# A dense expert stage: the last weight grid stored by halves of its tokens, and plain fp32 output products in its first eight rounds

## The chip, the cores and the metric

The kernel runs on one NeuronCore of one Trainium2 chip. The metric is the device time of one execution in microseconds (us). Engines are named as in the profile: PE (TensorE matmuls), PEld (its weight loads), DVE (VectorE), ACT (ScalarE), POOL (GpSimd), SP (SyncE, which here only issues transfers).

## What is computed

One layer of a hybrid backbone for 1024 latent and 256 context tokens: attention, a gated recurrence, and then a feed-forward layer of product-key experts (PEER). Only the last part is touched. It is, for x of 1280 tokens by 1024:

```
def peer_ffn(x, w_q, sub_keys, u, v):
    ...
    expert = (idx1 * N_KEYS + idx2).reshape(N, PEER_HEADS * PEER_TOPK)
    g = jax.nn.softmax(best, axis=-1).astype(x.dtype).reshape(N, PEER_HEADS * PEER_TOPK)
    def one_chunk(args):
        x_c, e_c, g_c = args
        act = jax.nn.gelu(jnp.einsum('cd,ced->ce', x_c, u[e_c]), approximate=False)
        return jnp.einsum('ce,ced->cd', g_c * act, v[e_c])
```

Each token picks 8 x 16 = 128 of 128 x 128 = 16384 experts. u and v hold one row of 1024 fp32 for each expert.

## The kernel before

The kernel treats tokens in tiles of 128. Four tiles (512 tokens) go the **dense** way: every token is multiplied with all 16384 experts, and a grid of weights, mostly zero, makes the sum right. The other six tiles go the **gathered** way: for each of a token's 128 experts, POOL gathers a row of u (512 KB for 128 tokens), DVE takes the dot product with x, and later a row of v is gathered and multiplied in. Both ways run side by side in `experts`.

`place_weights` makes the dense grid: for each of four tiles t, in 8 steps of 16 tokens, 128 x 128 products on PE, copied by ACT into `grid[t % 2]` (64 KB per partition, partition = first key). A full tile (8 MB) is stored to the scratch tensor g in DRAM; `placed` counts ACT's copies, 32 for a tile. Tiles 0 to 2 are stored by SP (L2177), each when its tile is complete. The last tile is stored when complete: keys 0 to 3 by SP (L2179, semaphore `g_first`), keys 4 to 127 by ACT (L2170, `g_rest`). The block ends with a barrier over all engines, before which SP waits for the stores whose buffers are to be reused.

`experts` runs 64 rounds and an end. Round r treats experts n = 2r and 2r + 1 of each partition (a **pair**, e = 0, 1):

- PE: two products A (24 matmuls each, `a_ps`, L2395), each 8 slices k in three parts (hi x hi, hi x lo, lo x hi) of numbers that were split into two fp32r halves; then the output product O of the pair of round r - 1 (L2417), token tile by token tile, t = 0 to 3, into two PSUM buffers `o_ps[t % 2]`, also in three parts: 12 matmuls a tile.
- ACT: the high halves of v (L2455) and u (L2435), the Gelu of A into `hidden` (L2460), the high half of the weighted hidden, w (L2463).
- DVE: `weigh` (hidden times g_raw, L2635), the low halves of u and v (`split`, L2541) and of w (L2640), the additions of the four O tiles into `acc` (`add_tile`, L2657), and between these the dot products (L2580). The order is written out by hand: round r adds tiles 2 and 3 of O(r - 2) at its start and tiles 0 and 1 of O(r - 1) at its end. PE waits for `added` before it overwrites a PSUM buffer, so O's tile 2 waits for the addition of tile 0.
- SP, in order: v (2r), u (2r + 2), v (2r + 1), g_raw (r), u (2r + 3), 512 KB each. A load of v waits for the split of the v before in the same buffer (`v_ready`), g for both `weigh` of the round before (`weighted`), u for the split of the u before.
- POOL: the gathers; a row's buffer is free after its dot product.

Rounds 0 to 7 have mode "keys": 12 dot products each, over 4 rows of `key_row` and, from round 1 on, 8 of `value_row`. Rounds 8 to 63 have 8 gathered keys (or values) and 8 gathered value rows each, which PE multiplies in (L2381). In round 1, ACT, DVE, POOL and SP wait for `g_rest`, because the buffers of round 1 lie where `grid1` lay.

In what follows, T is the moment in which DVE has added tile 0 of O(r - 1), at the end of round r.

## Time and profile before

| | us |
|---|---|
| median of 3 runs | 3499.54 |
| lowest, highest | 3494.69, 3509.21 |
| span of the profiled execution | 3554.5 |

The profiled execution is 55 us (1.6%) longer than the median. All durations below are from it. Its first 1661 us lie before `experts`; the keys rounds end at 1917.0; rounds 8 to 63 take the time up to about 3510, and a closing normalisation the rest. The profile gives for each engine the busy time and, for each idle stretch, what ended it. Matmuls are pipelined: one of 512 columns is listed with 0.39 us but starts 0.227 us after the last.

### The profile page before, as it was taken

Reading aid. Unit: us, or ns where it says so; the run is one execution under the profiler, and the core shown is the slowest. Engines: PE = TensorE matmul, PEld = TensorE weight load, DVE = VectorE, ACT = ScalarE, POOL = GpSimd, SP = SyncE. Lnnn points to the kernel's source line nnn. Section 1 sums busy time; section 2 is a strip of 40 time slices with the busy share of each in tenths; the row PEclk is TensorE's granted clock in tenths of the full one; section 3 lists DMA queues with packets and bytes.
Section 4 is the critical chain, followed back from the end, with each engine's and each line's share of the span. In section 5 each row is a group of like instructions: output and inputs, shape, how many; then the busy total and the mean of one; then the engine's idle time right before and its main releaser. Section 6 shows DMA issues by size and latency. Waiting matters only on the chain. (4 is left out here: it accounts for less than half of the span.)

```text
span 3554.5 us, 46828 instructions
## 1 busy us (share of the span) xinstructions
PE 3102.6 (87%) x15159; PEld 2086.1 (59%) x15159; DVE 2701.3 (76%) x5989; ACT 1072.9 (30%) x1920; POOL 1925.0 (54%) x1678
## 2 busy tenths in 40 slices
PE   6879999589889996676588999999899999999994
PEld 4647346366464443565466666667676667666663
DVE  2328788797578998898688778777787778787777
ACT  4731344365111110677122222222222222222222
POOL 0000466454345566553665667677667666766673
PEclk9979999799999998898799999999999999999997
DMA  9432788776867889799988999999999999999996
GB/s 331 155 123 74 239 273 263 209 228 208 313 237 244 298 297 327 248 404 340 358 325 299 389 397 385 403 410 399 368 405 401 403 385 410 393 409 378 369 394 261
DMA packets 366664, 1133.22 MB, mean 319 GB/s; under 512 B 33017, under 2 KB 91641, under 8 KB 366385
## 3 DMA queue, kind: packets, MB, share of 16 engines
q0 software_dynamic: 221184, 805.40, 60.5%
q1 hardware_dynamic: 136832, 314.44, 23.9%
q10 hardware_dynamic: 8496, 11.50, 0.9%
q8 instruction: 78, 1.28, 0.1%
q14 instruction: 74, 0.60, 0.1%
HBM read 1077.51 MB, written 53.71 MB: 318 GB/s over the span
## 5 line engine op out<-in xcount | busy, mean ns | idle before, releaser
L403 POOL DMA_INDIRECT ahead_row<-in_u_rows,keep_tables x256 | 339.1, 1325 | 669.8 <-POOLq L102 371.7
L2525 POOL DMA_INDIRECT exp_value_row<-in_v_rows,exp_v_id x448 | 585.0, 1306 | 169.7 <-issue 140.0
L2514 POOL DMA_INDIRECT edge_row<-in_u_rows,edge_u_id x424 | 459.2, 1083 | 345.1 <-DVE edge_dot L2580 165.0
L2417 PE MATMUL exp_o_ps<-exp_v_hi,exp_w_hi 128*128 128x512 f32 x1024 | 337.5, 412 | 104.2 <-DVE keep_acc L2657 101.0
L2395 PE MATMUL exp_a_ps<-exp_xT_hi,exp_u_hi 128*128 128x512 f32 x1024 | 409.0, 399 | 20.8 <-DVE exp_u_lo L2541 11.0
L2395 PE MATMUL exp_a_ps<-exp_xT_lo,exp_u_hi 128*128 128x512 f32 x1024 | 402.0, 393 | 0.5 <-issue 0.3
L2395 PE MATMUL exp_a_ps<-exp_xT_hi,exp_u_lo 128*128 128x512 f32 x1024 | 401.4, 392 | 0.8 <-issue 0.8
L2580 DVE CUSTOM_DVE_ANT_0 edge_row<-edge_row,keep_tables 128x1024 f32<-128x1024 f32 x256 | 313.2, 1224 | 103.6 <-DMA edge_row<-in_u_rows,edge_u_id 81.7
L2657 DVE TENSOR_TENSOR keep_acc<-exp_o_ps,keep_acc 128x1024 f32<-128x1024 f32 x256 | 312.0, 1221 | 94.8 <-PE exp_o_ps L2417 78.6
L413 DVE CUSTOM_DVE_ANT_0 ahead_row<-ahead_row,ahead_x 128x1024 f32<-128x1024 f32 x256 | 305.9, 1220 | 84.6 <-DMA ahead_row<-in_u_rows,keep_tables 83.6
L2417 PE MATMUL exp_o_ps<-exp_v_lo,exp_w_hi 128*128 128x512 f32 x1024 | 327.5, 402 | 0.0
L2417 PE MATMUL exp_o_ps<-exp_v_hi,exp_w_lo 128*128 128x512 f32 x1024 | 325.7, 400 | 0.0
L2417 PEld LDWEIGHTS exp_o_ps<-exp_v_hi,exp_w_hi 128*128 128x128 f32 x1024 | 194.4, 196 | 198.1 <-DVE keep_acc L2657 152.1
L2580 DVE CUSTOM_DVE_ANT_0 edge_row<-edge_row,edge_x 128x1024 f32<-128x1024 f32 x168 | 204.7, 1223 | 69.5 <-DMA edge_row<-in_u_rows,edge_u_id 57.8
L2395 PEld LDWEIGHTS exp_a_ps<-exp_xT_hi,exp_u_hi 128*128 128x128 f32 x1024 | 193.8, 189 | 108.2 <-issue 47.5
L2381 PE MATMUL exp_v_ps<-exp_value_row,exp_hot 128*32 128x512 f32 x1792 | 219.0, 600 | 40.0 <-DMA exp_value_row<-in_v_rows,exp_v_id 20.0
L2455 ACT ACTIVATE exp_v_hi<-exp_v_raw 128x1024 fp32r<-128x1024 f32 x128 | 135.0, 1055 | 381.8 <-PE exp_o_ps L2417 225.6
L2460 ACT ACTIVATE exp_hidden<-exp_a_ps 128x512 f32<-128x512 f32 x128 | 76.6, 599 | 562.8 <-PE exp_a_ps L2395 448.4
L1483 PE MATMUL queries_q_ps<-mix_featT,queries_slab 128*128 128x512 f32 (+1 forms) x640 | 231.1, 514 | 0.0
L2417 PEld LDWEIGHTS exp_o_ps<-exp_v_lo,exp_w_hi 128*128 128x128 f32 x1024 | 199.8, 195 | 44.8
L2417 PEld LDWEIGHTS exp_o_ps<-exp_v_hi,exp_w_lo 128*128 128x128 f32 x1024 | 199.1, 194 | 44.2
L2395 PEld LDWEIGHTS exp_a_ps<-exp_xT_hi,exp_u_lo 128*128 128x128 f32 x1024 | 193.8, 189 | 43.4 <-issue 1.8
(420 smaller groups left out, 5716.2 us busy)
## 6 DMA issues: line engine op xcount, KB each, us to landing
exp_v_raw<-in_v_rows SPq DMA_DIRECT2D x128, 512.0 KB
edge_u_raw<-in_uT SPq DMA_DIRECT2D x128, 512.0 KB
exp_g_raw<-scratch_g SPq DMA_DIRECT2D x64, 512.0 KB
scratch_g<-place_grid SPq DMA_DIRECT2D x3, 8192.0 KB
proj_ctx_mod_slab<-in_w_mod SPq DMA_DIRECT2D x8, 2048.0 KB, 13.2
heads_early_room<-in_w_in SPq DMA_DIRECT2D x10, 1024.0 KB, 11.8
mod_slab<-in_w_mod SPq DMA_DIRECT2D x4, 2048.0 KB, 21.3
queries_slab<-in_w_q SPq DMA_DIRECT2D x4, 2048.0 KB, 26.2
```

What stands on the lines that cost most here:

```text
L403: nc.gpsimd.indirect_dma_start(out=ahead.row[:, n % KEY_RING, :], out_offset=None, in_=io["u_rows"], in_offset=bass.IndirectOffsetOnAxis(a ...
L413: nc.vector.tensor_tensor_reduce(out=row, in0=row, in1=ahead.x[:, n // SLOTS - ahead.first, :], scale=1.0, scalar=0.0, op0=ALU.mult, op1=A ...
L1483: last = nc.tensor.matmul(q_ps[:, 0:width], slab[:, k, ct * P:(ct + 1) * P], h2T[:, k, at:at + width], start=(k == 0), stop=(k == KD - 1))
L2381: mm = nc.tensor.matmul(v_ps[QUAD * t:QUAD * (t + 1), half * SLAB:(half + 1) * SLAB], hot[:, i % 2, t, :], value_row[:, 4 * (i % 2) + t, h ...
L2395: mm = nc.tensor.matmul(a_ps[e][:, :], u[part][:, e, k, :], xT[xp][:, k, :], start=(k == 0 and part == 0 and xp == 0), stop=(k == KD - 1 a ...
L2417: mm = nc.tensor.matmul(o_ps[t % 2][:, c, :], w[1 - parity][part][:, e, t * P:(t + 1) * P], v[1 - parity][xp][:, e, c * SLAB:(c + 1) * SLA ...
L2455: nc.scalar.activation(v[parity][0][:, e, :], v_raw[:, e, :], ACT.Copy).then_inc(v_hi_ready, 1)
L2460: nc.scalar.activation(hidden[:, e, :], a_ps[e][:, :], ACT.Gelu).then_inc(hidden_ready, 1)
L2514: nc.gpsimd.indirect_dma_start(out=row, out_offset=None, in_=io["u_rows"] if mode != "last" else io["v_rows"].rearrange("a b n -> (a b) n" ...
L2525: nc.gpsimd.indirect_dma_start(out=value_row[:, 4 * (j % 2) + t, :], out_offset=None, in_=io["v_rows"].rearrange("a b n -> (a b) n"), in_o ...
L2580: nc.vector.tensor_tensor_reduce(out=row, in0=row, in1=x, scale=1.0, scalar=0.0, op0=ALU.mult, op1=ALU.add, accum_out=dot[:, parity, j:j + ...
L2657: nc.vector.tensor_tensor(acc[:, t, :], o_ps[t % 2][:, :, :].rearrange("p c n -> p (c n)"), acc[:, t, :], ALU.add).then_inc(added, 1)
```

## The change

Four things are changed together.

1. **The last tile's grid is stored by halves of its tokens.** Within a grid the order of elements is now (pair r, half of tokens h, e, token), and for the last tile (h, r, e, token). SP stores tokens 0 to 63 after half of the last tile's copies, as 512-byte pieces; after the last copy, tokens 64 to 127 go out, pairs 0 and 1 by SP, the rest by ACT. SP also waits for the first half's store (`half_stored`) ahead of the barrier.
2. **Buffers are laid out anew.** What rounds 0 to 7 use lies outside the second half of `grid1`; the buffers first used in round 8 (v_raw, the low halves) lie over it. The waits for `g_rest` of ACT, DVE and POOL in round 1 are gone; SP's stays, after the loads of round 1.
3. **The output products of rounds 0 to 7 are plain fp32.** v is loaded to `v_whole[parity]`, `weigh` writes `w_whole[parity]`, and O has 4 plain matmuls a tile in place of 12 fp32r ones. The splits of v and w fall away in these rounds. SP's load of v waits, from round 2 on, for `o_made >= 4 (r - 1)`: for all four tiles of O(r - 2), which read the same buffer.
4. The first A product waits for the slices of xT one by one, and the zeroing of `acc` moves behind the first `weigh`.

```diff
-FIRST_KEYS = 4
-REST_KEYS = ((FIRST_KEYS, N_KEYS),)
+FIRST_PAIRS = 2
...
+            sp.wait_ge(placed, LAST_TILE * PER_TILE + PER_TILE // 2)
+            sp.dma_start(half_target(0, 0, N_KEYS // 2), half_grid(0, 0, N_KEYS // 2)).then_inc(half_stored, 16)
             sp.wait_ge(placed, DENSE_TILES * PER_TILE)
-            sp.dma_start(place(DENSE_TILES - 1, 0, FIRST_KEYS), placed_keys(1, 0, FIRST_KEYS)).then_inc(edge.g_first, 16)
+            sp.dma_start(half_target(1, 0, FIRST_PAIRS), half_grid(1, 0, FIRST_PAIRS)).then_inc(edge.g_first, 16)
             sp.wait_ge(stored[0], 32)
             sp.wait_ge(stored[1], 16)
+            sp.wait_ge(half_stored, 16)
...
                 for e in range(PAIR):
                     n = 2 * r + e
-                    if at_least(r, 1):
+                    if mode == "keys":
+                        if e == 0 and at_least(r, 2):
+                            sp.wait_ge(o_made, DENSE_TILES * (r - 1))
+                        target = v_whole[parity][:, e, :]
+                    else:
                         sp.wait_ge(v_ready, n - 1)
-                    sp.dma_start(v_raw[:, e, :], io["v_rows"][:, n, :]).then_inc(v_in[e], 16)
+                        target = v_raw[:, e, :]
+                    sp.dma_start(target, io["v_rows"][:, n, :]).then_inc(v_in[e], 16)
...
-            pe.wait_ge(xT_ready, 1)
...
+                            if isinstance(r, int) and n == 0:
+                                pe.wait_ge(xT_ready, k + 1)
...
+                            for c in range(2) if whole else ():
+                                mm = nc.tensor.matmul(
+                                    o_ps[t % 2][:, c, :], w_whole[1 - parity][:, e, t * P:(t + 1) * P],
+                                    v_whole[1 - parity][:, e, c * SLAB:(c + 1) * SLAB], start=(e == 0), stop=(e == 1))
...
-                if isinstance(r, int) and r == 1:
-                    act.wait_ge(edge.g_rest[0], 16)
...
-                        if isinstance(r, int) and r == 1 and j == RING:
-                            pool.wait_ge(edge.g_rest[0], 16)
...
                 def split_v(e):
-                    if not last:
+                    if not last and not wide:
```

On PE, behind the A products of round 1, the output product of round 0 (4 token tiles). Before, one tile of the four is six rows of two matmuls:

```order
712 L2417 MATMUL exp_o_ps<-exp_v_hi,exp_w_hi 128x512 x2
713 L2417 MATMUL exp_o_ps<-exp_v_lo,exp_w_hi 128x512 x2
714 L2417 MATMUL exp_o_ps<-exp_v_hi,exp_w_lo 128x512 x2
715 L2417 MATMUL exp_o_ps<-exp_v_hi,exp_w_hi 128x512 x2
716 L2417 MATMUL exp_o_ps<-exp_v_lo,exp_w_hi 128x512 x2
717 L2417 MATMUL exp_o_ps<-exp_v_hi,exp_w_lo 128x512 x2
```

Now the four tiles together are one row, between the last A matmul and the loop:

```order
710 L2423 MATMUL exp_a_ps<-exp_xT_hi,exp_u_lo 128x512
...
712 L2456 MATMUL exp_o_ps<-exp_whole_v,exp_whole_w 128x512 x16
713 L2296 UNCONDITIONAL_BRANCH
```

48 matmuls of split operands have become 16 plain ones.

On DVE, a keys round of the loop from the fourth dot product (a dot product is two rows, ISA) to the second u split. Before:

```order
2292 L2635 TENSOR_TENSOR exp_hidden<-exp_hidden,exp_g_raw 128x512
2293 L2580 ISA exp_value_row,edge_dot<-exp_value_row,edge_x 128x1024
...
2295 L2640 TENSOR_TENSOR exp_w_lo<-exp_hidden,exp_w_hi 128x512
2296 L2541 TENSOR_TENSOR exp_u_lo<-edge_u_raw,exp_u_hi 128x1024
...
2304 L2541 TENSOR_TENSOR exp_v_lo<-exp_v_raw,exp_v_hi 128x1024
...
2306 L2635 TENSOR_TENSOR exp_hidden<-exp_hidden,exp_g_raw 128x512
...
2309 L2640 TENSOR_TENSOR exp_w_lo<-exp_hidden,exp_w_hi 128x512
2310 L2541 TENSOR_TENSOR exp_u_lo<-edge_u_raw,exp_u_hi 128x1024
```

and now:

```order
2282 L2676 TENSOR_TENSOR exp_whole_w<-exp_hidden,exp_g_raw 128x512
2283 L2621 ISA exp_value_row,edge_dot<-exp_value_row,edge_x 128x1024
...
2285 L2585 TENSOR_TENSOR exp_u_lo<-edge_u_raw,exp_u_hi 128x1024
...
2293 L2676 TENSOR_TENSOR exp_whole_w<-exp_hidden,exp_g_raw 128x512
...
2296 L2585 TENSOR_TENSOR exp_u_lo<-edge_u_raw,exp_u_hi 128x1024
```

The two splits of w and the two of v are gone (the first split of v stood further ahead); nothing else has moved.

On SP, from the stores to the loads of round 0. Before:

```order
91 L2177 DMA scratch_g<-place_grid 128x64x256 x3
92 L2179 DMA scratch_g<-place_grid 128x2x256
93 L102 UNCONDITIONAL_BRANCH
```

and now, with the half of the last tile as a row of its own:

```order
91 L2193 DMA scratch_g<-place_grid 128x64x256 x3
92 L2195 DMA scratch_g<-place_grid 128x64x128
93 L2197 DMA scratch_g<-place_grid 128x2x128
94 L102 UNCONDITIONAL_BRANCH
```

The loads of each round behind them stand in the same order as before (v, u, v, g, u), the first of each round now behind the wait for `o_made`.

## Rows read from the trace of the kernel before

**Rows 1.** Page: span, and busy time of each engine.
```profile
span 3554.5 us, 46828 instructions
PE 3102.6 (87%) x15159; PEld 2086.1 (59%) x15159; DVE 2701.3 (76%) x5989; ACT 1072.9 (30%) x1920; POOL 1925.0 (54%) x1678
```
**Rows 2.** Busy time by stretch: rounds 2 to 7, round 8, later rounds.
```profile
core 0: us, PE busy (x) PEld busy (x) DVE busy (x) ACT busy (x) POOL busy (x), PEclk, DMA share, GB/s
1746.30:1917.00 170.70, 143.46 (x578) 115.76 (x577) 152.53 (x217) 39.56 (x54) 106.19 (x79) 0.92 0.85 315
...
1917.00:1944.30 27.30, 26.67 (x116) 20.34 (x116) 21.95 (x33) 6.59 (x9) 15.46 (x15) 0.92 1.02 404
...
2100.00:3300.00 1200.00, 1135.63 (x5504) 818.20 (x5504) 928.25 (x1285) 278.81 (x387) 828.08 (x773) 0.99 1.00 396
```
**Rows 3.** Timeline, ACT: the Gelu of the dots, which ends rounds 0, 1, 7.
```profile
1705.70 0.21 ACT L2470 ACTIVATE edge_act_row<-edge_dot 128x12 f32<-128x12 f32 x1 [7.82 <-DVE edge_dot L2580]
...
1746.32 0.21 ACT L2470 ACTIVATE edge_act_row<-edge_dot 128x12 f32<-128x12 f32 x1 [5.76 <-DVE edge_dot L2580]
...
1917.03 0.21 ACT L2470 ACTIVATE edge_act_row<-edge_dot 128x12 f32 x1 [5.84 <-DVE edge_dot L2580]
```
**Rows 4.** Timeline, DVE, end of round 4 and round 5.
```profile
1831.40 1.22 DVE L2657 TENSOR_TENSOR keep_acc<-exp_o_ps,keep_acc 128x1024 f32<-128x1024 f32 x1
1835.93 1.23 DVE L2657 TENSOR_TENSOR keep_acc<-exp_o_ps,keep_acc 128x1024 f32<-128x1024 f32 x1 [3.30 <-PE exp_o_ps L2417]
...
1841.10 1.22 DVE L2541 TENSOR_TENSOR exp_v_lo<-exp_v_raw,exp_v_hi 128x1024 fp32r<-128x1024 f32 x1
...
1845.67 0.69 DVE L2635 TENSOR_TENSOR exp_hidden<-exp_hidden,exp_g_raw 128x512 f32<-128x512 f32 x1
...
1847.42 0.69 DVE L2640 TENSOR_TENSOR exp_w_lo<-exp_hidden,exp_w_hi 128x512 fp32r<-128x512 f32 x1
...
1858.36 1.22 DVE L2657 TENSOR_TENSOR keep_acc<-exp_o_ps,keep_acc 128x1024 f32<-128x1024 f32 x1
```
**Rows 5.** Timeline, PE, the same rounds, then one later gap (round 10).
```profile
1830.40 1.22 PE L2417 MATMUL exp_o_ps<-exp_v_hi,exp_w_hi 128*128 128x512 f32 x2 [4.54 <-DVE keep_acc L2657]
...
1835.69 0.81 PE L2417 MATMUL exp_o_ps<-exp_v_hi,exp_w_hi 128*128 128x512 f32 x2
...
1838.61 0.39 PE L2395 MATMUL exp_a_ps<-exp_xT_hi,exp_u_hi 128*128 128x512 f32 x1
...
1849.49 0.62 PE L2417 MATMUL exp_o_ps<-exp_v_hi,exp_w_hi 128*128 128x512 f32 x2
...
2000.82 1.22 PE L2417 MATMUL exp_o_ps<-exp_v_hi,exp_w_hi 128*128 128x512 f32 x2 [3.39 <-DVE keep_acc L2657]
```
**Rows 6.** Groups by shape, PE: plain fp32 matmuls of 512 columns, two records each.
```profile
L1337 PE MATMUL queries_q_ps<-out_lat_w,mix_featT 128*128 128x512 f32 x256 | 114.4, 608 | 10.0 <-DMA out_lat_w<-in_w_out 10.0
```
**Rows 7.** Timeline, SP: v and g for round 2.
```profile
1739.45 0.33 SPq L2340 DMA_DIRECT2D exp_v_raw<-in_v_rows  x1
1740.06 0.33 SPq L2346 DMA_DIRECT2D exp_g_raw<-scratch_g  x1
```
**Rows 8.** Transfers: size, median us from issue to landing; the first alone, the others beside gathers.
```profile
out_ctx_w<-in_w_out SPq DMA_DIRECT2D x2, 2048.0 KB, 10.4
...
keep_acc<-scratch_h2T ACTq DMA_DIRECT2D x1, 2048.0 KB, 9.6
...
queries_slab<-in_w_q SPq DMA_DIRECT2D x1, 2048.0 KB, 14.2
...
scratch_g<-place_grid ACTq DMA_DIRECT2D x1, 7936.0 KB, 59.7
```
**Rows 9.** Timeline, DVE and SP: the wait in round 1, the store's issue.
```profile
1720.97 0.37 DVE L2664 COPY exp_pair_first<-keep_iota 64x16 f32<-64x16 f32 x2 [15.39 <-DMA scratch_g<-place_grid]
...
1661.25 0.37 SPq L2179 DMA_DIRECT2D scratch_g<-place_grid  x1
```
**Rows 10.** DMA, 1648 to 1656: GB/s in 40 slices; queue, packets, MB, share.
```profile
GB/s 379 379 394 389 374 389 389 384 369 389 333 287 333 307 338 333 317 389 251 287 333 451 410 369 348 348 246 164 184 184 123 82 102 20 0 0 0 0 0 0
...
q1 hardware_dynamic: 1018, 1.03, 36.8%
```
**Rows 11.** DMA, 1740 to 1960: the same queue.
```profile
q1 hardware_dynamic: 5760, 20.97, 26.2%
```
**Rows 12.** DMA, 1661.25 to 1746.3: all packets.
```profile
DMA packets 14157, 30.06 MB, mean 353 GB/s; under 512 B 680, under 2 KB 8872, under 8 KB 14154
```
**Rows 13.** Timeline, ACT: its first instruction behind the barrier.
```profile
1662.73 1.06 ACT L2435 ACTIVATE exp_u_hi<-edge_u_raw 128x1024 fp32r<-128x1024 f32 x1 [1.50 <-PEq L2366]
```

More of the change, by code:

```diff
@@ L394, in __init__ @@
         self.g_first = signals.sem("edge_g_first")
-        self.g_rest = [signals.sem(f"edge_g_rest{n}") for n in range(len(REST_KEYS))]
+        self.g_rest = signals.sem("edge_g_rest")
         self.early_in = signals.sem("edge_early_in")
@@ L1927, in place_weights @@
             .rearrange("p (t n) c -> p t n c", t=DENSE_TILES)
-        grid = [s.sb(f"grid{n}", [P, N_KEYS, P]) for n in range(2)]
+        grid = [s.sb(f"grid{n}", [P, N_KEYS * P]) for n in range(2)]
         KEYS = range(CONTEXT_GATHER * SLOTS, CONTEXT_GATHER * SLOTS + PLACE_DOTS)
@@ L2168, in _ @@
             act.wait_ge(placed, DENSE_TILES * PER_TILE)
-            for n, (lo, hi) in enumerate(REST_KEYS):
-                nc.scalar.dma_start(place(DENSE_TILES - 1, lo, hi), placed_keys(1, lo, hi)).then_inc(edge.g_rest[n], 16)
+            nc.scalar.dma_start(half_target(1, FIRST_PAIRS, N_KEYS // 2), half_grid(1, FIRST_PAIRS, N_KEYS // 2))\
+              .then_inc(edge.g_rest, 16)
         @block.sync
@@ L2224, in experts @@
         hot = s.sb("hot", [P, 2, 4, QUAD])
+        value_row = s.sb("value_row", [P, VALUE_RING, D])
+        v_raw = s.sb("v_raw", [P, 2, D])
+        for parity in range(2):
+            v[parity].append(s.sb(f"v_lo{parity}", [P, PAIR, D], FP32R))
+            w[parity].append(s.sb(f"w_lo{parity}", [P, PAIR, TOK], FP32R))
         a_ps = [s.psum(f"a_ps{n}", [P, SLAB]) for n in range(2)]
@@ L2409, in body @@
                     g = r - 1
-                    pe.wait_ge(w_ready, 2 * g + 2 + 2)
-                    pe.wait_ge(v_ready, 2 * g + 2)
+                    whole = mode == "keys" or isinstance(r, int) and r == FIRST
+                    if whole:
+                        pe.wait_ge(weighted, 2 * g + 2)
+                        for e in range(PAIR):
+                            pe.wait_ge(v_in[e], 16 * g + 16)
+                    else:
+                        pe.wait_ge(w_ready, 2 * g + 2 + 2)
+                        pe.wait_ge(v_ready, 2 * g + 2)
                     for t in range(DENSE_TILES):
@@ L2414, in body @@
                         for e in range(PAIR):
-                            for part, xp in ((0, 0), (0, 1), (1, 0)):
+                            for part, xp in () if whole else ((0, 0), (0, 1), (1, 0)):
                                 for c in range(2):
@@ L2458, in body @@
                     act.wait_ge(a_made, n + 1 + 2)
[L2459 removed]
+                    if mode == "keys":
+                        if at_least(r, 1):
+                            act.wait_ge(weighted, n - 1)
+                    else:
+                        if isinstance(r, int) and r == FIRST:
+                            act.wait_ge(weighted, n - 1)
+                        act.wait_ge(w_ready, n - 1 + 2)
                     nc.scalar.activation(hidden[:, e, :], a_ps[e][:, :], ACT.Gelu).then_inc(hidden_ready, 1)
                     split_u(n + 2, e, r + 1)
[L2462 to L2463 removed]
+                    if mode != "keys":
+                        act.wait_ge(weighted, n + 1)
+                        nc.scalar.activation(w[parity][0][:, e, :], hidden[:, e, :], ACT.Copy).then_inc(w_hi_ready, 1)
                 keys = key_units(r, mode) if mode != "last" else []
@@ L2565, in body @@
                 last = mode == "end"
+                wide = mode == "keys"
                 def dot_product():
@@ L2643, in split_v @@
                 def split_v(e):
-                    if not last:
+                    if not last and not wide:
                         split(v[parity][1][:, e, :], v_raw[:, e, :], v[parity][0][:, e, :], v_hi_ready, v_ready, 2 * r + e)
```

82 lines of the change are left out of this document (47 added, 35 removed).

## The prediction

> **What bounds the kernel now.** I read the page first [rows 1]: a long span, no engine saturated over the whole of it. So I went to the busy time by stretch [rows 2]. From round 8 on, DMA is busy all the time at about 400 GB/s and PE for 95%; whatever the change moves ahead of round 8 shifts that part but doesn't shorten it. In rounds 2 to 7 no resource is full: 170.7 us for six rounds, 28.45 us a round, DVE 152.5 us busy (25.4 a round), PE 143.5, DMA 0.85. The ends of rounds [rows 3] give the start: round 0 ends at 1705.7, round 1 at 1746.3, and between lies a stall in which DVE waited 15.4 us for the grid's store [rows 9].
>
> A round in the timelines of DVE and PE [rows 4, 5]: DVE adds tile 0 (done at 1830.3, just ahead of PE's start at 1830.40); PE has idled 4.5 us for that and begins O's tile 2. It starts at the low clock: records are 0.427 us apart (1.2 GHz; six pairs from 1830.40 to 1835.69 are 0.43 us a matmul), later 0.227 us (2.4 GHz; 48 A matmuls from 1838.61 to 1849.49). DVE, done with tile 1, waits 3.3 us for tile 2. Then it runs without a pause to the next addition of tile 0. So the loop is: T, tiles 2 and 3 on PE, DVE's work, next T. **DVE's chain and its handover with PE bind, not PE's work.**
>
> **Part by part: the output products.** A plain fp32 matmul of 512 columns costs 114.4 us / 128 = 0.894 us [rows 6] (256 records, two to each), that is, four times the 0.227 us of an fp32r one. The split product had three. O costs 16 x 0.90 = 14.5 us a round in place of 48 x 0.227 = 10.9: **PE gets 3.6 us more**. A tile costs 3.6 us at the full clock and 6.8 at the low one. PE's round is then 10.9 + 14.5 = 25.4 us.
>
> **The splits.** DVE loses two of 1024 (pitch 1.13 us) and two of 512 columns (0.60): 3.5 us a round [rows 4]. ACT loses 2 x 0.95 + 2 x 0.6 us; it is idle most of the time, so this counts nothing. If that were all, the round would be bound by PE at about 25.4 us, with DVE at 25.4 - 3.5 = 21.9 and DMA at 28.45 x 0.85 = 24.2 us of full share.
>
> **The new wait on SP.** It is where I part from that. v, u, v, g, u stand in one queue. Before, g for round 2 was issued at 1740.1 [rows 7], ahead of the round's start at 1746. Now all five stand behind `o_made >= 4 (r - 1)`, which comes when PE has finished tile 3 of O(r - 2), after T. g is the fourth, and DVE needs it for the first `weigh`, five dot products into the round; all of DVE's round is queued behind that. In order from T:
> - PE's tiles 2 and 3: at the full clock 7.3 us. PE will have idled first (below), and 3.4 to 4.5 us of idling left it at the low clock [rows 5]. The low clock lasted 5.3 us from 1830.40 (and 3.3 in the next round); 4.3 us of it hold 10 of the 32 passes of 0.427, the other 22 take 5.0: 9.3 us.
> - SP's wake-up: 0.2 us.
> - Four loads of 512 KB to the landing of g. 2048 KB took 9.6 us next to a store and gathers, and 14.2 us beside gathers [rows 8]. Below, at the 410 GB/s of a busy moment, 2.1 MB take 5.1 us, and some 2 us of issue and landing come on top: 7. I take 10, close to the 9.6 because its packets and its neighbours are most alike, and keep 7 and 14.2.
> - DVE from `weigh` to the end of the addition of tile 0: 1858.36 - 1845.67 + 1.22 = 13.9 us, less a split of v and two of w (2.3): 11.6 us.
>
> Sum: 9.3 + 0.2 + 10 + 11.6 = **31.1 us a round, 2.7 more than before**. PE then idles 31.1 - 9.3 - 18.2 = 3.6 us (18.2: both A and tiles 0 and 1), which bears out the low clock. Six rounds (2 to 7): **+16**. With 7 us: PE hardly idles, its clock stays up, 7.3 + 0.2 + 7 + 11.6 = 26.1 a round, -14. With 14.2: 35.3, +41.
>
> Here the Trainium skill has a rule ("DMA: Bandwidth & Descriptors", section "Queues, rings and completion order"): a DMA engine goes round-robin between the queues that have work, packet by packet. If the gathers always have work, SP's queue gets half. By that estimate, half of 410 GB/s gives 10.2 us for the 2.1 MB and 12.2 with the fixed part, a round of 33.3 us and +29 instead of +16. No row here shows how the two share in these rounds; the 9.6 us row speaks for less.
>
> **Round 8** still makes O(7) plain, and O(6)'s last tiles: +3.6 us for PE, which was busy for 26.7 of 27.3 us there [rows 2]. Its loads aren't held. I take +3, from 0 to 4.
>
> **The start.** The last store began at 1661.25 [rows 9] and landed 59.7 us later [rows 8]. The DMA queues were empty from about 1654.6 on [rows 10], the last of the 40 slices with more than nothing. The first half, issued at about 1636 behind tile 2's store on the same queue, can use that time. It has 8192 packets of 512 bytes. A packet of 1012 bytes mean costs 46 ns of an engine's time [rows 10] (0.368 x 16 x 8 us / 1018), one of 3641 bytes 160 [rows 11]: the line through both gives 25 ns at 512, from which 8192 x 25 / 16 = 12.8 us for the half; the bounds are 23 (in proportion) and 46 ns (no cheaper). By 1662.5 it has had 7.9 us; the other 4.9 are shared with the second half on ACT's queue and take twice that: 1672.3, and 1.5 us to land. SP waits for it ahead of the barrier, and every engine is queued behind that. `experts` starts at about 1675 in place of 1662.7 [rows 13]. The gain must come after that. Round 0 has about 28 us of DVE work (12 dots at 1.15, the xT slices 5.0, four splits of u at 1.13, the zeroing 3.5, two `weigh` at 0.6) and waits for gathers in a ring of four; round 1, without the stall, has 19.5 us, and took 25.3 with its splits from 1721.0. 32 + 23 give 1730. DMA says the same: 30.06 MB moved from 1661.25 to 1746.3 [rows 12]; of these 4.2 are moved ahead, 1.5 of the second half by 1675, and about 1 (v and g of round 2) is asked for later: 23.4 MB at 410 GB/s are 57 us, 1732. I take 1731 for the end of round 1: **-15**. Bounds: 23 ns a packet gives -17; 46 ns gives a start at 1697 and +6. If the barrier were not late at all, DMA alone would give -22. The slices of xT (4.4 us earlier for the first A) are hidden behind the gathers, at nothing; without that cover they gain 4. ACT's grid copies have the same elements in the same short runs, and DVE was full in that stage: nothing.
>
> **Sum.** 3554.5 - 15 + 16 + 3 = 3558.5 for the profiled execution, which stood 55 us above the median; all terms are shifts, so the median moves likewise: 3499.5 + 4 = **3503.5**. Below, "same" means within 0.5% (17.5 us), about what can be told from no change.
>
> **Rivals.**
> 1. **The loads are in time, PE binds.** If g lands by 7.5 us or so, PE hardly pauses, its clock stays up, and a round takes 25.4 to 26: -17 here, in all 3499.5 - 15 - 17 + 3 = 3470. For it: DMA has 15% of slack, and while DVE waits it asks for no gathers. Against it: five loads at once, just as the gathers of the last dots are under way. Chance 0.2.
> 2. **The held queue costs more** (the slower side): SP's loads behind `o_made` land g at 14.2 us, as the row beside gathers had it; 35.3 us a round, 3499.5 - 15 + 41 + 3 = 3528. It decides from a landing of 12.3 us on, where the sum passes +17.5. Chance 0.2 (with the skill's round-robin rule at its edge, 3516).
> 3. **512-byte packets are no cheaper than 1 KB ones.** The barrier opens 34 us late; 3499.5 + 6 + 16 + 3 = 3524.5. For it: no packet of that size was in the trace. Chance 0.05.
> 4. **A plain matmul needs fewer passes here than in [rows 6].** With two, tiles 2 and 3 take 5.5 us, a round 27.3 (-7): 3480. Chance 0.03.
>
> The forecast has 0.52. It spreads to both sides by its unknown landing: 0.46 of it within 0.5%, 0.03 below, 0.03 above. Faster: 0.2 x 0.85 + 0.03 + 0.02 = 0.22; slower: 0.2 + 0.04 + 0.03 = 0.27; same: 0.51. The range takes in rivals 1 and 2 but for their ends: 3468 to 3532.
>
> **What would show it.** (a) The ends of rounds 2 to 7 lie 31 us apart. (b) In each, DVE waits 4 to 5 us before the first `weigh`, for a DMA of g. (c) SP issues v, u, v, g, u in a burst some 9 us after T, and PE idles 3 to 4 us ahead of tile 2 and starts it at the low clock. (d) SP's wait for the half store ends near 1674, and round 1 ends near 1731, with no stall of 15 us. (e) From round 8 on everything is shifted and nothing else. If rounds come at 25 to 26 us with PE busy throughout, the landing was mis-sized; if round 1 ends after 1740, the half store was.

## The result, and the profile after

The changed kernel takes 3522.53 us (median of 9 runs, 3509.19 to 3524.39); the kernel before took 3499.54 (9 runs beside them). The ratio is 1.0047, 95% interval [1.0033, 1.0061]: slower by 12 to 21 us. On the chip of the last four experiments the changed kernel was run once more and gave 1.0032 [1.0016, 1.0048]. The forecast was 3503.5 within 3468 to 3532, "same" within 0.5% (17.5 us): the time lies in the range, and above the forecast by 19 us. Whether it is "same" or "slower" by that bound, the interval of 12 to 21 us doesn't decide.

The page of the changed kernel, for [rows 1]:

```profile
span 3522.5 us, 46488 instructions
PE 3110.2 (88%) x15031; PEld 2041.9 (58%) x15031; DVE 2673.4 (76%) x5957; ACT 1047.9 (30%) x1888; POOL 1913.5 (54%) x1678
```

The spans mislead: 3522.5 is less than the 3554.5 of before. The ends of the rounds say where that comes from. In the timeline of ACT, the Gelu of the dots (line 2470 before, now 2515) closes rounds 0 to 8; for [rows 3]:

```profile
1712.90 0.21 ACT L2515 ACTIVATE edge_act_row<-edge_dot 128x12 f32<-128x12 f32 x1 [19.64 <-DVE edge_dot L2621]
1734.83 0.21 ACT L2515 ACTIVATE edge_act_row<-edge_dot 128x12 f32<-128x12 f32 x1 [18.42 <-DVE edge_dot L2621]
1771.22 0.21 ACT L2515 ACTIVATE edge_act_row<-edge_dot 128x12 f32 x1 [9.39 <-DVE edge_dot L2621]
1803.51 0.21 ACT L2515 ACTIVATE edge_act_row<-edge_dot 128x12 f32 x1 [9.54 <-DVE edge_dot L2621]
1834.73 0.21 ACT L2515 ACTIVATE edge_act_row<-edge_dot 128x12 f32 x1 [9.55 <-DVE edge_dot L2621]
...
1927.74 0.21 ACT L2515 ACTIVATE edge_act_row<-edge_dot 128x12 f32 x1 [9.27 <-DVE edge_dot L2621]
1956.63 0.21 ACT L2515 ACTIVATE edge_act_row<-edge_dot 128x8 f32<-128x8 f32 x1 [5.76 <-DVE edge_dot L2621]
```

Counted between marks inside each trace, before against after:

| stretch | before | after | difference |
| --- | --- | --- | --- |
| start to the issue of the last store | 1661.25 | 1654.08 | -7.2 |
| last store's issue (1661.25; 1654.08) to end of round 1 | 85.1 | 80.75 | -4.3 |
| rounds 2 to 7 | 170.7 | 192.9 | +22.2 |
| round 8 | 27.3 | 28.9 | +1.6 |
| end of round 8 to end of the span | 1610.2 | 1565.9 | -44.3 |

The first line and the last are not the change. The 7.2 us were there before the grid's first tile was stored (issued at 1500.5 and 1492.8; from there to the last store 160.7 and 161.3 us). In the rounds behind round 8 nothing differs, and the execution of before that was profiled stood 55 us above its median. The three lines between give +19.5, which agrees with the +16 of the ratio and the +23 of the medians.

Busy time by stretch, for [rows 2]: last store's issue to the end of round 0, round 1, round 2, rounds 3 to 7, round 8, later rounds (columns as there):

```profile
1654.08:1712.90 58.82, 24.60 (x91) 19.47 (x92) 28.68 (x41) 10.99 (x16) 16.13 (x17) 0.71 0.94 322
1712.90:1734.83 21.93, 9.40 (x24) 4.47 (x23) 19.19 (x31) 3.19 (x5) 17.27 (x13) 0.76 0.85 284
1734.83:1771.22 36.39, 27.22 (x82) 15.92 (x81) 22.11 (x33) 3.53 (x5) 24.98 (x22) 0.88 0.97 357
1771.22:1927.74 156.52, 135.46 (x401) 79.02 (x401) 110.09 (x161) 17.40 (x26) 70.17 (x60) 0.93 0.77 275
1927.74:1956.63 28.89, 28.89 (x97) 16.13 (x97) 22.09 (x33) 6.46 (x9) 16.63 (x16) 0.91 1.01 392
2100.00:3300.00 1200.00, 1161.87 (x5655) 832.92 (x5656) 952.32 (x1312) 287.92 (x398) 855.82 (x794) 1.00 1.02 406
```

In rounds 3 to 7 DVE works 22.0 us of 31.3 (it was 25.4 of 28.45) and DMA's share fell from 0.85 to 0.77: the splits are gone, the work is less, and the round is longer. What it waits for stands in the timelines of DVE, SP and PE at the end of round 3 and in round 4, for [rows 4, 5, 7]:

```profile
1800.95 1.22 DVE L2700 TENSOR_TENSOR keep_acc<-exp_o_ps,keep_acc 128x1024 f32<-128x1024 f32 x1
...
1821.82 0.69 DVE L2676 TENSOR_TENSOR exp_whole_w<-exp_hidden,exp_g_raw 128x512 f32<-128x512 f32 x1 [4.92 <-DMA exp_g_raw<-scratch_g]
...
1832.17 1.22 DVE L2700 TENSOR_TENSOR keep_acc<-exp_o_ps,keep_acc 128x1024 f32<-128x1024 f32 x1
...
1811.24 0.33 SPq L2367 DMA_DIRECT2D exp_whole_v<-in_v_rows  x1
1811.83 0.33 SPq L2349 DMA_DIRECT2D edge_u_raw<-in_uT  x1
1812.35 0.33 SPq L2367 DMA_DIRECT2D exp_whole_v<-in_v_rows  x1
1812.88 0.65 SPq L2373 DMA_DIRECT2D exp_g_raw<-scratch_g  x1
1813.73 0.55 SPq L2349 DMA_DIRECT2D edge_u_raw<-in_uT  x1
...
1790.66 7.03 PE L2456 MATMUL exp_o_ps<-exp_whole_v,exp_whole_w 128*128 128x512 f32 x16
1802.22 8.83 PE L2456 MATMUL exp_o_ps<-exp_whole_v,exp_whole_w 128*128 128x512 f32 x16 [4.54 <-DVE keep_acc L2700]
```

Read it as the loop: tile 0 is added by 1802.2 (T); PE, idle for 4.5 us, makes tiles 2 and 3 by 1811.0; only then does SP issue its five loads; g lands for the `weigh` at 1821.8, DVE having waited 4.9 us; the next T is 11.6 us later, at 1833.4. The waits from the end of round 1 to that of round 7 (engine, line, what was waited for: us in total, times, longest):

```profile
DVE exp_whole_w L2676 <- DMA exp_g_raw<-scratch_g: 32.1, 6, 9.5
```

At the start, the timelines of SP and POOL, then the waits of SP (columns as above), for [rows 9, 13]:

```profile
1629.34 13.01 SPq L2195 DMA_DIRECT2D scratch_g<-place_grid  x1
1654.08 9.55 SPq L2197 DMA_DIRECT2D scratch_g<-place_grid  x1
...
1669.99 0.19 POOL L2533 COPY edge_u_id<-keep_tables 128x12 int32<-128x12 int32 x1 [43.27 <-POOLq L102]
```

```profile
SPq L2200 <- DMA scratch_g<-place_grid: 5.9, 1, 5.9
```

The stall of 15.4 us in round 1 is gone, but SP's issue of the second half's first pairs was held for 9.6 us and the wait for the first half for 5.9, so in `experts` ACT's first instruction comes 16.6 us after the last store's issue and not 1.5 (POOL's, the row above, 15.9 and not 0.9).

### The profile page after: what moved, and what is told of

Same layout as the page of the kernel before. It is cut to its first block and busy times, and to the rows that moved or that the text cites. A ratio compares the mean times of both kernels' runs of the same rounds, so it can differ in the third digit from the quotient of the medians.

```text
span 3522.5 us, 46488 instructions
## 1 busy us (share of the span) xinstructions
PE 3110.2 (88%) x15031; PEld 2041.9 (58%) x15031; DVE 2673.4 (76%) x5957; ACT 1047.9 (30%) x1888; POOL 1913.5 (54%) x1678
## 5 line engine op out<-in xcount | busy, mean ns | idle before, releaser
L2451 PE MATMUL exp_o_ps<-exp_v_hi,exp_w_hi 128*128 128x512 f32 x896 | 287.6, 402 | 15.4 <-DVE keep_acc L2700 15.0
L2451 PE MATMUL exp_o_ps<-exp_v_hi,exp_w_lo 128*128 128x512 f32 x896 | 283.6, 397 | 0.0
L2451 PE MATMUL exp_o_ps<-exp_v_lo,exp_w_hi 128*128 128x512 f32 x896 | 281.3, 395 | 0.0
L2504 ACT ACTIVATE exp_hidden<-exp_a_ps 128x512 f32<-128x512 f32 x128 | 76.6, 599 | 630.3 <-PE exp_a_ps L2423 630.2
L2451 PEld LDWEIGHTS exp_o_ps<-exp_v_hi,exp_w_hi 128*128 128x128 f32 x896 | 163.6, 188 | 101.4 <-DVE keep_acc L2700 65.8
L2423 PEld LDWEIGHTS exp_a_ps<-exp_xT_hi,exp_u_lo 128*128 128x128 f32 x1024 | 193.0, 188 | 41.2
L2423 PEld LDWEIGHTS exp_a_ps<-exp_xT_lo,exp_u_hi 128*128 128x128 f32 x1024 | 193.2, 189 | 39.7 <-issue 1.7
L2493 ACT ACTIVATE exp_v_hi<-exp_v_raw 128x1024 fp32r<-128x1024 f32 x112 | 118.1, 1055 | 311.2 <-PE exp_o_ps L2451 295.6
L475 POOL DMA_INDIRECT val_row<-in_v_rows,keep_tables x136 | 145.2, 1068 | 116.0 <-PE route_lat_h_ps L489 64.4
## 6 DMA issues: line engine op xcount, KB each, us to landing
proj_ctx_mod_slab<-in_w_mod SPq DMA_DIRECT2D x8, 2048.0 KB, 12.9
```

What stands on the lines that cost most here:

```text
L475: nc.gpsimd.indirect_dma_start(out=val.rows[slot][:, t, :], out_offset=None, in_=io["v_rows"].rearrange("a b n -> (a b) n"), in_offset=bas ...
L2423: mm = nc.tensor.matmul(a_ps[e][:, :], u[part][:, e, k, :], xT[xp][:, k, :], start=(k == 0 and part == 0 and xp == 0), stop=(k == KD - 1 a ...
L2451: mm = nc.tensor.matmul(o_ps[t % 2][:, c, :], w[1 - parity][part][:, e, t * P:(t + 1) * P], v[1 - parity][xp][:, e, c * SLAB:(c + 1) * SLA ...
L2493: nc.scalar.activation(v[parity][0][:, e, :], v_raw[:, e, :], ACT.Copy).then_inc(v_hi_ready, 1)
```

## The experiments

The theory LATE G: the loop above, T to g to `weigh` to T, sets rounds 2 to 7, because SP's loads stand behind the end of the output product. For the start three things were open: the barrier, the bytes, and the zeroing of the accumulator in its new place. Times are ratios to the kernel before on the same chip. There were three chips, whose times differ by up to 70 us for one kernel and are not to be mixed in us: g_ahead, g_first, held_before and warm ran on the first, open_start, g_last, memset_back and best on the second, and open_back, best_again, g_ahead_again and after_again, the changed kernel itself, on the third. On the first two the changed kernel did not run, so there its times stand in only by its ratio. Rounds are read from the same rows of ACT as above, and the start from the issue of the last store.

### g_ahead: the loads issued ahead of T

```
 for rounds >= 2 of the first eight, on SP:
+    load_u(2 * r + 2, 0); load_u(2 * r + 3, 1)
+    sp.wait_ge(v_in[0], 16 * r)
+    load g
     sp.wait_ge(o_made, DENSE_TILES * (r - 1))
     load v 0
+    sp.wait_ge(v_in[1], 16 * r)
     load v 1
```

> The changed kernel, but in rounds 2 to 7 SP issues both loads of u and the load of g ahead of its wait for o_made, and only the two loads of v behind it (v_in waits keep two loads of one buffer apart). Theory LATE G (rounds 3 to 7 of the changed kernel are 31.3 us because g lands 10.5 us after the wait is over and DVE is queued behind it): DVE's wait for g goes away, PE's own 25.4 us bind, rounds of 25.5 to 26.5 us, 28 to 38 us less in all, a ratio to the kernel before of 0.993 to 0.997. Rival SLOW PE (the plain products and the low clock after PE's pause set the round, the held loads are beside it): rounds stay at 30 us or more, ratio 1.003 to 1.006.

Measured: 0.9919 [0.989, 0.9947]. In its trace, the busy time of its rounds 3 to 7, then DVE's first `weigh` of one of these rounds:

```profile
1762.01:1887.00 124.99, 124.64 (x401) 75.01 (x400) 110.06 (x161) 16.54 (x26) 86.22 (x64) 1.00 0.94 356
```

```profile
1824.09 0.69 DVE L2688 TENSOR_TENSOR exp_whole_w<-exp_hidden,exp_g_raw 128x512 f32<-128x512 f32 x1 [0.40 <-ACT exp_hidden L2516]
```

Five rounds in 125.0 us, 25.0 each, with PE busy for 124.6 at a full clock: g is no longer waited for, and PE binds. That is more than was expected of it (rounds of 25.5 to 26.5, a ratio of 0.993 to 0.997). This is the largest effect of the study: the order of one queue was worth 6.3 us a round, where the splits had cost DVE 3.4.

### g_first and g_last: the place of g in the burst

```
 g_first: after the wait for o_made:  g, v, u, v, u
 changed kernel:                      v, u, v, g, u
 g_last:                              v, u, v, u, g
```

> The changed kernel, with all five loads of rounds 2 to 7 still behind the wait for o_made, but g the first of them in place of the fourth (g, v, u, v, u). Theory LATE G: one load of 512 KB lands in 4 to 5 us in place of 10.5; the first u is now the third and is wanted some 2 us after g; rounds of 26.5 to 28.5 us, ratio 0.996 to 1.000. Rival SLOW PE: rounds stay near 31 us, ratio 1.003 to 1.006.

> The changed kernel with only the order of SP's five 512-KB loads of a round changed in rounds 2 to 7: values, u, values, u and g last (it was fourth). All five are still issued from T on. What is tested: whether the landing of g, the largest term of the sum, goes by its place in SP's queue. Theory IN ORDER (g lands when what stands ahead of it has passed, 2.0 MB then, 2.5 MB now, at the some 200 GB/s that the queue gets beside the gathers): landing 10.5 -> about 13, round 31.2 -> 33.5 to 34, time about 14 us above the changed kernel (ratio to the kernel before 1.008 to 1.010). Rival SHARED (the loads that are open share the engines and land nearly together, so that the place does not matter): landing 10.5 to 11.5, round 31.2 to 32, time within 5 us of the changed kernel.

Measured: g_first 0.9938 [0.9905, 0.997], rounds 3 to 7 of 29.1, 29.4, 28.9, 26.7 and 25.4 us; g_last 1.0107 [1.0067, 1.0147], rounds 3 to 6 of 33.65, 33.9, 34.3 and 33.9. The first load and the first `weigh` of round 4, in g_first and then in g_last:

```profile
1805.41 0.33 SPq L2362 DMA_DIRECT2D exp_g_raw<-scratch_g  x1
...
1812.87 0.69 DVE L2693 TENSOR_TENSOR exp_whole_w<-exp_hidden,exp_g_raw 128x512 f32<-128x512 f32 x1 [1.79 <-DMA exp_g_raw<-scratch_g]
```

```profile
1818.22 0.33 SPq L2359 DMA_DIRECT2D exp_whole_v<-in_v_rows  x1
...
1831.04 0.69 DVE L2694 TENSOR_TENSOR exp_whole_w<-exp_hidden,exp_g_raw 128x512 f32<-128x512 f32 x1 [7.16 <-DMA exp_g_raw<-scratch_g]
```

From the burst's first issue to the `weigh`: 7.5 us as first, 10.6 as fourth (1811.24 to 1821.82), 12.8 as fifth. So the loads land in the order of issue: IN ORDER holds and SHARED falls, the step from fourth to fifth being 2.2 us for 512 KB. In g_first the round shrank by 2 to 6 us, not to the 25 of g_ahead: in round 4 DVE then waited 2.9 us for the split of the u that stands two places behind g in the burst. ACT's half of that split began 11.1 us after the burst's first issue, and 5.7 after the Gelu of the A product that it also waits for (0.5 in g_ahead). The profile names PE for that wait, but PE's product had long been done, so it was most likely the load: the burst, not g alone, is late.

### warm: PE kept busy through the gap

```
+    after tile 1 of O in rounds 1 to 7, on PE:
+        20 fp32r matmuls of 512 columns into an unused part of PSUM
```

> The changed kernel, with 20 more fp32r matmuls of 512 columns (4.5 us, into a PSUM tile that nobody reads in these rounds) behind tile 1 of each output product of rounds 0 to 7, so that PE doesn't pause before tile 2. If the low clock after the pause is a term of the chain (9.0 us for tiles 2 and 3 in place of 7.3), a round gets 1.7 us shorter: 29.6 us, some 10 us less in all, ratio 1.001 to 1.003. If the clock doesn't matter, or falls regardless: 31.3 us, ratio 1.004 to 1.006.

Measured: 1.0004 [0.9971, 1.0036]; rounds 4 to 6 of 29.3, 29.4, 29.6 us, PE's granted clock 1.00 in rounds 4 and 5 (0.93 in the changed kernel's rounds 3 to 7). The timelines of PE and DVE, round 4:

```profile
1812.44 7.13 PE L2457 MATMUL exp_o_ps<-exp_whole_v,exp_whole_w 128*128 128x512 f32 x16 [0.36 <-issue]
...
1830.12 0.69 DVE L2680 TENSOR_TENSOR exp_whole_w<-exp_hidden,exp_g_raw 128x512 f32<-128x512 f32 x1 [4.71 <-DMA exp_g_raw<-scratch_g]
```

Tiles 2 and 3 take 7.1 us in place of 8.8, and the round is shorter by 1.8, while the wait for g stays. The low clock after the gap is a term of its own in the chain of 31 us, and the smaller one. The times alone would not show this, since the interval reaches from 0.997 to 1.004; the rounds do.

### held_before: the wait alone, in the kernel before

```
+    if mode == "keys" and e == 0 and at_least(r, 2):
+        sp.wait_ge(o_made, DENSE_TILES * (r - 1))
-    if at_least(r, 1):
+    elif at_least(r, 1):
         sp.wait_ge(v_ready, n - 1)
```

> The kernel before with one edit: in rounds 2 to 7 SP's first load of v waits for o_made >= 4 (r - 1), as in the changed kernel; products and splits stay as they were. Theory LATE G: 8.4 us for tiles 2 and 3 at the split price, 0.2, 10.5 for the landing of g, 13.9 of DVE: rounds of about 33 us, 4.5 more than before, +27 us, ratio 1.006 to 1.010. Rival SLOW PE: no product became longer, so rounds stay at 28.5 us and the ratio at 1.000.

Measured: 1.0071 [1.0048, 1.0093]; rounds 2 to 7 take 38.0, 34.8, 32.3, 33.3, 31.9 and 32.3 us in place of 28.45. Its waits in rounds 3 to 6:

```profile
ACT exp_v_hi L2457 <- DMA exp_v_raw<-in_v_rows: 42.8, 4, 11.3
```

Rounds 3 to 7 average 32.9 us: the wait costs 4.5 us a round with splits and buffers as they were. So the plain products did not lengthen the round; the queue that they were fed by did. Under the same wait, the changed kernel's rounds of 31.3 us are 1.6 shorter. Here v was late rather than g, since it has a split in front of it.

### open_start, memset_back and both: the start

```
 open_start, SP at the end of the place stage:
-    sp.wait_ge(half_stored, 16)          (ahead of the barrier)
 and ahead of SP's first load of g, and of POOL's fifth gather of round 1:
+    wait for half_stored
 the second half's first pairs are stored from ACT's queue, ahead of the rest
 memset_back, DVE:
+    memset(acc) ahead of the first dot product
-    memset(acc) after the first weigh of round 0
 open_back: both;   best: both, and g_ahead
```

open_start:

> The changed kernel, in which SP no longer waits for the end of the last tile's first-half store ahead of the barrier of the place stage; POOL waits for it just before the first gather whose buffer lies over those rows (round 1, the fifth of its key gathers), SP before its first load of g, and the second half's first pairs are issued from ACT's queue ahead of the rest. What is tested: why the stretch from the last store's issue to the end of round 1 gained 4.3 us (80.75 against 85.07) and not 15. Yardsticks: in the changed kernel POOL's first gather comes 15.9 us after that issue, round 0 ends 58.8 us after it, round 1 80.75; other variants whose start is the same give 77.6 to 81.7 for the latter. Theory BARRIER (the late barrier is the loss, the work behind it is free to follow): the first gather comes 1.5 to 3 us after the issue, round 0 ends at about 45, round 1 at about 67; time 13 to 14 us below the changed kernel. Rival BYTES (from the issue on the DMA engines are busy throughout with stores, gathers and loads that must all pass before round 0 can end, so an open barrier only lengthens their landings; the share of 0.91 to 1.06 in the windows 1650 to 1713 leaves some 4 us to win): first gather as early, but round 0 ends at 54 to 57 and round 1 at 76 to 79; time 2 to 5 us below. Rounds 2 to 7 keep 31 us each in both.

memset_back:

> The changed kernel with the zeroing of the accumulator (3.47 us of DVE) back where it was before the change, ahead of the first dot product, and not between the weighing and the last dots of round 0. What is tested: whether its new place, where it stops the dots while the ring of four gathers is full and the DMA falls to 0 GB/s for about 4 us, costs what it removes from the start. Theory COSTS: round 0 ends 3 to 4 us earlier, counted from the last store's issue (58.8 -> about 55), and no slice of some 4 us near 0 GB/s stands in it. Rival FREE (DVE's instructions between the barrier and the end of round 0 are the same in sum and the gathers fill the ring during the zeroing, so only its place changes): 58 to 60. The whole time can't tell 3 us; the profile is read.

open_back:

> open_start and memset_back together, and nothing of the loads' order of rounds 2 to 7 (so these stay at 31 us each). Alone, the open barrier brought the end of round 1 to 76.6 us after the last store's issue and the zeroing's old place to 76.1 (the changed kernel 80.75; others with its start 77.6 to 81.7), but the kernel 'best', which has both, had 67.1, as the theory BARRIER wanted. What is tested: which of two explanations holds. Theory TOGETHER (each edit alone leaves the other hole in the DMA's work: the wait for the barrier, or the stop of the dots): open_back ends round 0 at 44 to 47 and round 1 at 66 to 70. Rival BACKLOG (in 'open_start' SP's first load behind the barrier was blocked for 10.15 us because the first-half store was still 38 us from its issue when it ended, and g of round 0 came late: DVE waited 9.8 us for it; in 'best' the store had ended after some 29 us and that load took 0.34 us): what counts is how much of the first-half store is left when the barrier opens, so open_back goes with its own SP row: where that first load is again blocked for about 10 us, DVE waits some 10 us for g of round 0 and round 1 ends at 73 to 77 despite both edits. Time: 14 us below the changed kernel by TOGETHER, 5 to 7 by BACKLOG with a blocked load.

best:

> g_ahead, open_start and memset_back together: loads of u and g of round r issued ahead of T, the barrier of the place stage not held by the first-half store, the accumulator zeroed ahead of the first dot product. g_ahead alone gave 0.9919 [0.989, 0.9947] of the kernel before, with rounds of 25.0 us. Theory LATE G with BARRIER and COSTS: rounds 3 to 7 at 25.0 again, start 14 to 17 us shorter: 0.9919 - 0.004 to 0.005 = 0.987 to 0.988. With BYTES and FREE: start 2 to 5 us shorter, 0.9905 to 0.9915.

best_again:

> The kernel 'best' a second time, beside g_ahead and the changed kernel on the same chip, since the ratios of different chips leave 10 us open. If the start of 67 us is its own (TOGETHER), round 1 ends at 66 to 70 after the last store's issue again and the time is 8 to 12 us below g_ahead's. By BACKLOG it may fall back to 73 to 77, with a blocked first load in SP's rows, and the time lies within 5 us of g_ahead's. Rounds 3 to 7 at 25.0 in both.

g_ahead_again:

> The loads of u and g ahead of T once more: ratio to the kernel before 0.989 to 0.995, 28 to 32 us below the changed kernel on the same chip; rounds 3 to 7 at 25.0, round 1 ends 77 to 81 us after the last store's issue.

after_again:

> The changed kernel itself on the chip of these three, as the yardstick for them: ratio 1.003 to 1.007; round 1 ends 77 to 82 us after the last store's issue, rounds 3 to 7 at 31 us, round 2 at 36.

All from the issue of the last store, in us, but for "round 0", which is the time from ACT's first instruction in `experts` to the end of round 0. "SP held" is how long SP's first DMA issue behind the barrier lasted (0.34 when free), "g" how long DVE waited for g of round 0. (The 15.9 us that the first expectation calls POOL's first gather are its first instruction; the gather itself came at 17.0.)

| kernel | first gather | SP held | g | end of round 0 | end of round 1 | round 0 | GB/s to end of round 0 |
| --- | --- | --- | --- | --- | --- | --- | --- |
| before | 2.0 | 0.34 | 0 | 44.5 | 85.1 | 43.0 | 385 |
| changed | 17.0 | 0.34 | 0 | 58.8 | 80.75 | 42.2 | 322 |
| after_again | 15.8 | 0.34 | 0 | 57.6 | 79.9 | 42.2 | 327 |
| g_ahead, g_ahead_again | 12.0, 13.6 | 0.34 | 0 | 53.9, 55.2 | 77.6, 78.9 | 42.3, 42.0 | 346, 334 |
| g_last, g_first, warm | 12.9, 15.2, 19.0 | 0.34 | 0 | 54.6, 56.7, 59.7 | 77.6, 79.3, 81.7 | 42.1, 41.9, 41.2 | 340, 331, 316 |
| memset_back | 13.4 | 0.34 | 0 | 53.4 | 76.1 | 40.4 | 355 |
| open_start | 3.2 | 10.15 | 9.8 | 53.9 | 76.6 | 51.1 | 359 |
| open_back | 3.2 | 1.58 | 0 | 45.2 | 68.1 | 42.5 | 379 |
| best | 3.3 | 0.34 | 0 | 44.6 | 67.1 | 41.8 | 381 |
| best_again | 3.3 | 9.19 | 5.2 | 49.5 | 73.7 | 46.8 | 376 |

The rows on which it turns: SP's first load behind the barrier and a wait of DVE, in open_start, then the same two in best_again:

```profile
1659.54 10.15 SPq L2355 DMA_DIRECT2D keep_tables<-scratch_h  x1
```

```profile
DVE exp_whole_w L2677 <- DMA exp_g_raw<-scratch_g: 9.8, 1, 9.8
```

```profile
1649.22 9.19 SPq L2355 DMA_DIRECT2D keep_tables<-scratch_h  x1
```

```profile
DVE exp_whole_w L2691 <- DMA exp_g_raw<-scratch_g: 5.2, 1, 5.2
```

Opening the barrier alone brought the gathers 14 us forward and round 1's end only 4: BARRIER, as it was stated (the work behind an open barrier is free to follow), falls. BYTES forecast that, but falls with best and open_back: the bytes from the issue to the end of round 0 were 17.0 MB there in 44.6 us, and 18.9 in 58.8 in the changed kernel. The rate differs, so the start was not full. TOGETHER gave 68.1 for open_back, then missed best_again (66 to 70 expected, 73.7 measured), and that one had the held load that BACKLOG names. With single executions of each, roughly: zeroing back, both with a held load, 76.6 to 73.7, 3 us; the backlog, in best_again against best and open_back, 73.7 to 67.1 or 68.1, some 6 us; the barrier 4. The parts are not independent, since only an open barrier meets the backlog: without it, in open_back and best, round 1 ended 8 and 9 us earlier than in memset_back, for gathers 10 us earlier. memset_back alone, at 76.1, is hardly told from the kernels that have the changed kernel's start (77.6 to 81.7): inconclusive by itself. Its round 0 is the shortest of the table, by 1 to 2 us against those seven.

The column "round 0" says more. Wherever SP was held for less than 2 us, round 0 took 40 to 43 us, in the kernel before too. What moved its end was when it began.

The same store held SP also where the barrier waits for it. SP's issue of the second half's first pairs lasted 5.15 us in g_ahead and 11.5 in warm, the ends of the seven kernels with that start, and the first gather came 12.0 and 19.0 us after the last store's issue. What decides how much of the backlog is left wasn't controlled. The first half had been issued 24.9, 25.5, 26.0 and 26.4 us before the last store in open_start, best_again, open_back and best, and SP was held for 10.2, 9.2, 1.6 and 0.3 us: the order fits, no more.

In time: after_again 3516.9 us, open_back 3512.0 (1.0024 [1.0009, 1.0039]), g_ahead_again 3481.2 (0.9926 [0.9901, 0.9951]), best_again 3476.1 (0.9909 [0.9888, 0.993]) on one chip; best was 0.9928 [0.9902, 0.9955] on another. Both pairs differ by 5 us. The rows of the start say 12 for the first and 5 for the second; the intervals overlap in both, so a gain of the start is read in the traces, and isn't shown in the time. open_start gave 1.0038 [1.0017, 1.0058] on its chip, which isn't told from the changed kernel's 1.0047 either; memset_back has one run and no ratio.

Several of the expected times did not come out. best was to be at 0.987 to 0.988, and 0.9928 and 0.9909 were measured. open_back was to be 14 us below the changed kernel by TOGETHER, and was 5. g_ahead_again was to be 28 to 32 us below it, and was 36. best and g_ahead aren't told apart in time. Both are faster than the kernel before by 0.7 to 0.9%, and on the third chip than the changed kernel by 1.2% and 1.0%.

## Why the prediction was right or wrong, by its steps

**What binds.** Right. From T to T the prediction had 9.3 + 0.2 + 10 + 11.6 = 31.1 us. The rows of round 4 give 9.1 from T to the first issue, SP's wake-up among it, 10.6 to the `weigh`, 11.6 to the next T: 31.2 with rounding. Rounds 4, 5 and 6 took 31.2, 31.1 and 31.25. PE's gap was 4.5 us where 3.6 was expected; what was expected of its clock held (8.8 us for the two tiles where 9.3 was taken, 7.0 for two at the full clock). g_last and warm each moved one term, and the round by 2.5 and 1.8 us, held_before put the wait alone into the kernel before, and g_ahead took the loop away.

**The landing of g.** 10 was taken and 10.6 measured. It was chosen from rows of 9.6 and 14.2 us because the first looked most alike, and nothing in the trace of before could settle that; so some luck is in it. A landing of 15.1 us, beyond the slow end, was seen in round 2 of the changed kernel. Its first load was issued at 1743.17 and the `weigh` began at 1758.30, after a wait of 9.5 us:

```profile
1743.17 0.35 SPq L2367 DMA_DIRECT2D exp_whole_v<-in_v_rows  x1
...
1758.30 0.69 DVE L2676 TENSOR_TENSOR exp_whole_w<-exp_hidden,exp_g_raw 128x512 f32<-128x512 f32 x1 [9.49 <-DMA exp_g_raw<-scratch_g]
```

**Round 2** is the term that the rounds' sum lacked: 36.4 us, five more than the others, so +22.2 for the six and not +16. The queues' packets, bytes and shares show it, first for round 2 from 1742 to 1758, then for round 4 from 1811.2 to 1821.8:

```profile
q0 software_dynamic: 985, 3.60, 60.4%
q1 hardware_dynamic: 661, 2.44, 39.3%
```

```profile
q1 hardware_dynamic: 654, 2.42, 62.2%
q0 software_dynamic: 323, 1.19, 27.7%
```

SP's queue (q1) moved 2.4 MB in both. In round 2 three times as many bytes of gathers (q0) went beside it, at twice the rate. In round 4 the DMA engines stood idle when the burst came (0 GB/s from 1809.2 to 1811.2, against 296 from 1735 to 1742 in round 2). Our reading is that DVE's own wait of the round before had held the gathers back, and that round 2 had no such round ahead of it; no run tests this. The Trainium skill ("DMA: Bandwidth & Descriptors", section "Queues, rings and completion order") has each engine alternate between the queues that have work; where both had work, in round 2, the shares were 39 and 60%, which agrees roughly, though SP's queue got less than half and the landing, 15.1 us, was longer than the prediction's 12.2 by that rule. In the steady rounds the gathers had less work, and the 12.2 us and 33.3 us a round were not reached.

**Round 8.** +3 taken, +1.6 measured.

**The start** is the step that failed: -15 taken, -4.3 measured. The price of a packet was near: from 1662 to 1670 queue 10 passed 3930 of 512 bytes in 88% of the engines' time, 0.88 x 16 x 8 / 3930 = 28.7 ns, where 25 was taken. The barrier opened late by about what was expected: ACT's first instruction came 16.6 us after the last store's issue where 13.8 was taken, so only 3 us are lost there:

```profile
q10 hardware_dynamic: 3930, 2.01, 88.0%
```

What was mis-sized is round 0, "32 us" from the barrier: it took 42.2 (ACT's first instruction at 1670.67, end at 1712.90). The 32 were 28 us of DVE's work and 4 of waits for gathers. The work was right, 28.7 us. The waits were not; from the barrier to the end of round 0, before and then after:

```profile
DVE edge_row L2580 <- DMA edge_row<-in_u_rows,edge_u_id: 8.8, 6, 2.7
DVE edge_row L2621 <- DMA edge_row<-in_u_rows,edge_u_id: 11.6, 8, 2.1
```

In the kernel before, round 0 had taken 43.0 us, with 32.1 of DVE's work. The splits gave 3.4 us back and the waits for gathers took 2.8 of them. In best and open_back these waits were 11.1 and 11.7 us. The prediction had no row for the 4, and the trace before had 8.8.

Why the waits grew is only in part known. In round 0 of the changed kernel DMA moved 14.0 MB at 331 GB/s; at the 410 of a busy moment that would need 34 us. 512-byte packets passed at 290 GB/s until about 1673. And the change's own new place for the zeroing stopped DVE, with it the dots, and with those the ring of four gathers:

```profile
1694.20 3.47 DVE L2725 MEMSET keep_acc<- 128x4096 f32 x1 [0.80 <-issue]
```

From 1692 to 1704 DMA averaged 242 GB/s, 2 MB or 5 us short of 410. The prediction had counted the zeroing as 3.5 us of DVE's work and not asked what stood behind it. But the 5 us are not what it cost: with the zeroing back, in memset_back, round 0 was 1 to 2 us shorter, in one trace. The rest stays open. The prediction's second way, DMA's bytes at 410 GB/s, gave 70.8 us from the issue to the end of round 1; only kernels with the zeroing back, the barrier open and SP free came there (67.1 and 68.1, at 372 GB/s in best). Round 1 took 21.9 where 23 was taken.

**The sum.** The start missed by +10.7, rounds 2 to 7 by +6.2 and round 8 by -1.4, in all +15.5 on the forecast's +4: the 19.5 of the table. The two large misses have one sign, and nothing cancelled; the time stayed in the range because that was 64 us wide. The prediction had the mechanism of the rounds right and the size of the start wrong.

**The rivals.** (1) PE binds at 25.4: its condition, g in time, did not hold, and its price was right: g_ahead has 25.0. (2) The landing of 14.2: true of round 2 alone. (3) 46 ns a packet: excluded, 28.7. (4) Fewer passes: excluded, 16 matmul records, two to each matmul, in 7.03 us are 0.88 us each, [rows 6] again.

**The checks.** (a) held for rounds 3 to 7 (32.3, 31.2, 31.1, 31.25, 30.7) and not for round 2; (b) held, 4.8 to 5.0 us in rounds 3 to 6; (c) held; (d) failed in part: the half store's end came near and the stall of 15 us was gone, but round 1's end came 11 us late, counted from the issue. By the prediction's sign for that (after 1740; it is 1742 on the clock of before) the half store would have been mis-sized, and the sign misleads: it was round 0. (e) can't be read from these two traces, whose tails differ by 44 us. On the first chip the rounds behind round 8 took 1627.8 us with the code of before (held_before) and 1627.4 and 1627.0 with the changed code (g_ahead, warm), so there it holds. Item 4 of the change, the slices of xT, which the prediction put at nothing, was not tested by itself.

## What to carry to other kernels

When a change frees an engine, look at what the buffers' new release does to the queue that feeds it: here five loads in one queue got the wait of the latest of them, and that cost more than the work that was saved. A load is best issued by its own condition, and ahead of the loads whose buffers come free later. When an instruction is moved on an engine whose progress lets a short ring of gathers go on, ask what the ring loses as well as how long it lasts; here a zeroing of 3.5 us left a gap in the DMA's work, and moving it back gained some 1 to 3 us in single traces. And when a stretch is priced by an engine's work, look up in the trace how long that same stretch had taken, and what it waited for: round 0 had 8.8 us of waits where 4 were taken.
